# An encoder layer on one core: the experts' weights moved from the streamed to the split side of the matmuls

## The chip, the core and the metric

The kernel runs on one core of one Trainium2 chip. The metric is the device time of one execution in microseconds, the median of three runs. A core has five engines that work in parallel and meet at semaphores: TensorE (PE in the profile, with its weight loads as PEld), VectorE (DVE), ScalarE (ACT), GpSimd (POOL) and SyncE (SP), which here only issues transfers. In a matmul one operand is loaded into the array (stationary) and the other streams through it (moving). PSUM has eight banks of 128 x 512 float32.

## The reference, cut to what matters

One layer of an encoder for 1024 tokens of width 1024: RMSNorm, input projection, three token mixers, output projection, RMSNorm, then a mixture of 32 experts of which each token uses two, and a final RMSNorm. Only the experts are touched by the change:

```
def hierarchical_moe(h, rg_w, rg_b, re_w, re_b, e_gate, e_up, e_down):
    ...
    for e in range(N_EXPERTS):
        y = (jax.nn.silu(t @ e_gate[e]) * (t @ e_up[e])) @ e_down[e]
        out = out + combine[:, e:e + 1] * y
```

`t` is 1024 x 1024; `e_gate[e]` and `e_up[e]` are 1024 x 256, `e_down[e]` is 256 x 1024, all float32, 3 MB an expert.

## The kernel before, in words

Input projection, mixers and output projection come first. The output projection's rows are normalised (`normalise2`, L1223, one call for each of 8 tiles of 128 tokens), stored to HBM as `h2_rows`, transposed and multiplied with the router's weights `rw`. VectorE makes from the router's result two lists, `tok` and `dest`, with 80 slots (`CAP`) for each expert; unused slots point out of bounds and move nothing, so an expert has 64 rows on average (2 x 1024 / 32). An overflow path for experts with more than 80 rows follows the loop and is skipped when there are none.

Then the experts. The first four are written out, the other 28 run in loops of four (`Fori`) on every engine. For expert e:

- GpSimd copies a column of `tok` into `tokc` (L1584) and gathers up to 80 rows into `xg` (L1586). A column of `dest` is copied (L1597) and `ysb` is scattered to `y_d` (L1599) three experts behind.
- SyncE fetches the weights into a ring of four places: `wg`, `wu` when `gate_up` of the expert four before is done, `wd` when its `down` is done. Each 1 MB is one transfer. In `wg` and `wu` partition p holds rows p, 128+p, ...: eight pieces of 1 KB in HBM. In `wd` a piece is 4 KB.
- TensorE transposes the rows (`ex_transposes`, L759, 8 instructions), runs `down_split` of expert e-2 and then `gate_up` of e (L768). `gate_up` is in plain float32: the weights are stationary, 32 blocks of 128 x 128, and the 96 columns of `xT` move; each such product is two matmul instructions in the profile (64 for an expert). `down_split` works with split operands: float32 w is taken as w_hi + w_lo, both of type float32r, and hi x hi, hi x lo and lo x hi are summed. That is 12 instructions with an 80-column stationary `hThi_e` or `hTlo_e` and 512 moving columns of `wdhi` or `wdlo` (L787, L788, L792).
- ScalarE copies `xT` (L1016), half of the result rows (L1047), casts `wd` to `wdhi` (L1036, 2048 elements a partition) and does the Silu (L1020). VectorE copies the other half (L1380), makes `wdlo` = `wd` - `wdhi` (L1388), the gated product (L1372) and its two parts (L1394, L1396).

After the last scatter SyncE loads all rows of `y_d` back, VectorE adds them (L1421), and the final norm and the stores end the program.

## Time and profile before

| what | us |
|---|---|
| median of three runs (894.12 to 897.29) | 895.49 |
| the profiled execution: its own time | 892.98 |
| the profiled execution: span from first to last instruction | 891.0 |
| first row transposes of the experts to the last result in PSUM (L759 at 498.4, L792 ends at 841.8) | 343.4 |

The span starts at the first instruction and leaves out some 2 us around it. The profile's page gives busy time by engine, the granted TensorE clock in tenths of full speed, and the chain that ended last; the trace gives single instructions by start and length, what an engine waited for before them, and bandwidth by stretch. Matmuls are pipelined: the length of one (393 ns for L788) overlaps the next, and the distance of their starts is what one costs.

### The profile page before, as it was taken

The numbers are of one execution on the slowest core, as the hardware profiler recorded it, in microseconds if no ns is written. First come the engines' busy times: TensorE is split into PE (matmuls) and PEld (weight loads), VectorE is DVE, ScalarE is ACT, GpSimd is POOL, SyncE is SP. The second block draws the span as 40 slices with busy tenths as digits, with TensorE's granted clock in tenths as the row PEclk, the third lists the DMA queues.
The fourth block names the chain that finished last, engine by engine and source line by source line (L and its number), as shares of the span: only waits on it lengthen the run. The fifth ranks groups of instructions, "written<-read, shape, count | busy, mean of one in ns | idle before, by whom it ended". The sixth has DMA issues, their size and how long they took to land.

```text
span 891.0 us, 13079 instructions
## 1 busy us (share of the span) xinstructions
PE 771.9 (87%) x5022; PEld 641.3 (72%) x5022; DVE 373.1 (42%) x767; ACT 302.0 (34%) x539; POOL 329.7 (37%) x313
## 2 busy tenths in 40 slices
PE   3999999999977888999973599999999999999700
PEld 2788888866654554787873599999998899999600
DVE  5540000046768885412238233343333333333266
ACT  6211112145558887202220233333333333333222
POOL 2432256435556771501110123443433333442134
PEclk9999999979999999999995699999999999999955
DMA  8451112000010002426358189999999999996194
GB/s 273 108 151 48 47 48 71 1 0 1 2 48 0 1 1 76 137 69 219 113 172 300 38 258 335 351 349 351 348 349 350 347 342 347 350 352 231 40 370 195
DMA packets 111238, 160.21 MB, mean 180 GB/s; under 512 B 8304, under 2 KB 88656, under 8 KB 111072
## 3 DMA queue, kind: packets, MB, share of 16 engines
q1 hardware_dynamic: 104800, 142.78, 47.9%
q0 software_dynamic: 6400, 16.92, 5.9%
q8 instruction: 25, 0.41, 0.2%
q14 instruction: 13, 0.11, 0.0%
HBM read 144.99 MB, written 18.87 MB: 184 GB/s over the span
## 4 chain that ended last, share of the span: by engine, by line
PE 75%; DVE 9%; ACT 6%; DMA 4%; issue 3%; POOL 1%; SPq 1%; POOLq 0%; ACTq 0%; DVEq 0%
PE ps L768 26%; PE ps L583 6%; PE ps L585 6%; PE ps L584 6%; PE ps L788 3%; PE ps L787 3%; PE ps L792 3%; PE ps L623 3%; PE ps L759 2%; PE ps L648 2%; PE ps L707 2%; PE ps L709 2%; PE ps L708 2%; PE ps L664 2%; PE ps L670 2%
## 5 line engine op out<-in xcount | busy, mean ns | idle before, releaser
L768 PEld LDWEIGHTS ps<-xT,wg 128*128 128x128 f32 x1024 | 121.6, 195 | 5.9 <-ACT xT L1016 2.3
L768 PE MATMUL ps<-xT,wg 128*128 128x96 f32 x1024 | 121.4, 278 | 1.8 <-ACT xT L1016 1.8
L768 PE MATMUL ps<-xT,wu 128*128 128x96 f32 x1024 | 119.6, 275 | 0.0
L768 PEld LDWEIGHTS ps<-xT,wu 128*128 128x128 f32 x1024 | 116.9, 192 | 0.0
L1388 DVE TENSOR_TENSOR wdlo<-wd,wdhi 128x2048 fp32r<-128x2048 f32 x32 | 73.4, 2292 | 63.0 <-ACT wdhi L1036 63.0
L583 PE MATMUL ps<-hThi,whi 128*128 128x512 f32 x224 | 88.3, 394 | 4.2 <-DVE hTlo L1086 4.2
L585 PE MATMUL ps<-hThi,wlo 128*128 128x512 f32 x224 | 87.7, 392 | 0.0
L584 PE MATMUL ps<-hTlo,whi 128*128 128x512 f32 x224 | 87.7, 391 | 0.0
L1584 POOL COPY tokc<-tok 80x1 int32 (+1 forms) x32 | 54.1, 1689 | 42.7 <-DVE tok L1369 30.7
L1597 POOL COPY destc<-dest 80x1 int32 (+1 forms) x32 | 5.7, 178 | 166.7 <-DVE ysb L1380 166.7
L1536 POOL TENSOR_SCALAR pswa<-pswa,esum 128x384 f32<-128x384 f32 (+1 forms) x48 | 55.5, 1165 | 31.8 <-DVE esum L1173 31.4
L1020 ACT ACTIVATE sg<-ps 128x192 f32<-128x192 f32 x32 | 10.6, 330 | 154.2 <-PE ps L768 154.2
L1036 ACT CAST wdhi<-wd 128x2048 fp32r<-128x2048 f32 x32 | 60.7, 1897 | 0.0
L707 PE MATMUL ps<-wohi,oThi 128*128 128x512 f32 x128 | 50.9, 397 | 4.0 <-DVE oTlo L1205 3.6
L583 PEld LDWEIGHTS ps<-hThi,whi 128*128 128x128 f32 x224 | 42.4, 189 | 13.3 <-issue 4.7
L787 PE MATMUL ps<-wdhi,hThi_e 128*80 128x512 f32 x128 | 52.0, 406 | 0.0
L788 PE MATMUL ps<-wdlo,hThi_e 128*80 128x512 f32 x128 | 50.3, 393 | 0.0
L1372 DVE TENSOR_TENSOR hT<-sg,ps 128x192 f32<-128x192 f32 x32 | 11.4, 356 | 92.7 <-ACT sg L1020 92.7
L1153 DVE CUSTOM_DVE_ANT_0 pna<-ps,te 128x512 f32<-128x512 f32 x16 | 10.9, 688 | 93.6 <-PE ps L623 93.4
L709 PE MATMUL ps<-wohi,oTlo 128*128 128x512 f32 x128 | 49.9, 390 | 0.0
L708 PE MATMUL ps<-wolo,oThi 128*128 128x512 f32 x128 | 49.9, 390 | 0.0
L1380 DVE COPY ysb<-ps 80x512 f32<-80x512 f32 x32 | 22.0, 686 | 66.4 <-PE ps L792 66.4
(194 smaller groups left out, 1415.4 us busy)
## 6 DMA issues: line engine op xcount, KB each, us to landing
wg<-in_expert_w_gate SPq DMA_DIRECT2D x32, 1024.0 KB, 8.9
wu<-in_expert_w_up SPq DMA_DIRECT2D x32, 1024.0 KB, 12.7
wd<-in_expert_w_down SPq DMA_DIRECT2D x32, 1024.0 KB, 6.0
y<-expert_rows SPq DMA_DIRECT2D x16, 512.0 KB, 9.5
wraw<-in_w_in SPq DMA_DIRECT2D x14, 512.0 KB, 3.9
xin<-in_x SPq DMA_DIRECT2D x8, 512.0 KB, 5.6
xres<-in_x SPq DMA_DIRECT2D x16, 256.0 KB, 3.0
h_rows<-h SPq DMA_DIRECT2D x8, 512.0 KB, 2.7
```

What stands on the lines that cost most here:

```text
L583: nc.tensor.matmul(bank, whi[i % 2][:, k, :], hThi[:, k, cols], start=(k == 0), stop=False)
L584: nc.tensor.matmul(bank, whi[i % 2][:, k, :], hTlo[:, k, cols], start=False, stop=False)
L585: mm = nc.tensor.matmul(bank, wlo[i % 2][:, k, :], hThi[:, k, cols], start=False, stop=(k == KT - 1))
L707: nc.tensor.matmul(ps[:, g % 4, :], oThi[:, k, rows], wohi[n][:, k, :], start=(k == 0), stop=False)
L708: nc.tensor.matmul(ps[:, g % 4, :], oThi[:, k, rows], wolo[n][:, k, :], start=False, stop=False)
L709: mm = nc.tensor.matmul(ps[:, g % 4, :], oTlo[:, k, rows], wohi[n][:, k, :], start=False, stop=(k == KT - 1))
L768: mm = nc.tensor.matmul(ps[:, bank, f * COLS:(f + 1) * COLS], w[:, k, c0:c0 + P], xTu[:, k, :], start=(k == 0), stop=(k == KT - 1))
L787: nc.tensor.matmul(ps[0:CAP, b0 + n, :], hThi_e[par][:, j, :], wdhi[par][:, j, cols], start=(j == 0), stop=False)
L788: nc.tensor.matmul(ps[0:CAP, b0 + n, :], hThi_e[par][:, j, :], wdlo[slot][:, j, cols], start=False, stop=False)
L1036: nc.scalar.copy(wdhi[u % 2][:], wd[u][:]).then_inc(wdhi_done, 1)
L1388: nc.vector.tensor_tensor(wdlo[u][:], wd[u][:], wdhi[u % 2][:].bitcast(F32), ALU.subtract).then_inc(wdlo_done, 1)
L1536: gp.tensor_scalar(pbuf(u), pbuf(u), esum[:, u:u + 1], None, ALU.mult).then_inc(norm_p, 1)
```

## The change

The experts are written out, without loops, and all products are split:

- `gate_up`: the rows are stationary now, as `xThi` and `xTlo` (80 columns), and gate and up weights move together, 256 columns of each, into one bank. Three products for each of 8 chunks of k make 24 matmuls of 512 columns. The result has the tokens on partitions, so the gated product `hx` is transposed (`h_rows`, two instructions) ahead of `down`.
- The weights' high parts are cast by ScalarE into four units of 8 KB (`unit`): two for the halves of gate and up (`half_high`, chunks 0 to 3 and 4 to 7) and one for `wd` (`down_high`). `half_high(e, 0)` waits for `down` of e-3, `half_high(e, 1)` for the first half of `gate_up(e-1)`, `down_high(e)` for `gate_up(e)`. VectorE makes the low parts in the place of the raw weights (`half_low`, `down_low`).
- `down` runs one expert behind instead of two. ScalarE copies the whole result, 80 x 1024 (`rows_out`).
- d_model is laid out as 8p + k over partition p and chunk k: `e_gate` and `e_up` come in one piece of 8 KB for each partition, `rw` likewise, and `normalise2` writes its row permuted, reading with a step of 8 elements.
- GpSimd uses `tok` and `dest` directly as indices; no copies of columns.

The core of the diff:

```diff
-        wg = [at(f"wg{i}", [P, KT, DE], F32, eoff[i]) for i in range(RING)]
-        wu = [at(f"wu{i}", [P, KT, DE], F32, eoff[i] + 8 * KB) for i in range(RING)]
+        wgu = [at(f"wgu{i}", [P, 2, KT, DE], F32, eoff[i]) for i in range(RING)]
+        wgulo = [at(f"wgulo{i}", [P, 2, KT, DE], F32R, eoff[i]) for i in range(RING)]
         wd = [at(f"wd{i}", [P, 2, D], F32, eoff[i] + 16 * KB) for i in range(RING)]
+        wdlo = [at(f"wdlo{i}", [P, 2, D], F32R, eoff[i] + 16 * KB) for i in range(RING)]
+        unit = [at(f"unit{i}", [P, 2, 4 * DE], F32R, off) for i, off in enumerate((H + 56 * KB, W + 56 * KB, H + 24 * KB, V))]
...
+        xThi = [at(f"xThi{i}", [P, KT, CAP], F32R, TMP + 2560 * i) for i in range(2)]
+        xTlo = [at(f"xTlo{i}", [P, KT, CAP], F32R, (TMP + 5120, W + 53 * KB)[i]) for i in range(2)]
+        sg = at("sg", [CAP, DE], F32, TD + 32 * KB)
+        hx = at("hx", [COLS, DE], F32, TD + 33 * KB)
+        hThi_e = at("hThi_e", [P, 2, CAP], F32R, TD + 34 * KB)
+        hTlo_e = at("hTlo_e", [P, 2, CAP], F32R, TD + 34 * KB + 640)
...
+        def weight_unit(e, part):
+            return unit[(3 * e + (0, 1, 5)[part]) % 4]
+        def raw_half(w, e, a):
+            return w[e % RING][:, :, 4 * a:4 * a + 4, :].rearrange("p g k f -> p g (k f)")
...
-            sp.dma_start(rw[:, :, N_GROUPS:NR], re_w[0].rearrange("(k p) n -> p k n", p=P)).then_inc(const_in, 16)
+            sp.dma_start(rw[:, :, 0:N_GROUPS], rg_w[0].rearrange("(p k) n -> p k n", p=P)).then_inc(const_in, 16)
+            sp.dma_start(rw[:, :, N_GROUPS:NR], re_w[0].rearrange("(p k) n -> p k n", p=P)).then_inc(const_in, 16)
...
-                return (g_src.rearrange("(k p) f -> p k f", p=P), u_src.rearrange("(k p) f -> p k f", p=P),
+                return (g_src.rearrange("(p k) f -> p k f", p=P), u_src.rearrange("(p k) f -> p k f", p=P),
...
-            def fetch_expert(e, u, dynamic=False):
-                a, b, c = load_expert(e, u, dynamic)
-                if dynamic:
-                    sp.wait_ge(gu_done, e - (RING - 1))
-                sp.dma_start(wg[u][:], a).then_inc(wgu_in[u], 16)
-                sp.dma_start(wu[u][:], b).then_inc(wgu_in[u], 16)
-                if dynamic:
-                    sp.wait_ge(down_done, e - (RING - 1))
+            def fetch_expert(e):
+                u = e % RING
+                a, b, c = load_expert(e, u, False)
+                if e >= RING:
+                    sp.wait_ge(half_done, 2 * (e - RING) + 2)
+                sp.dma_start(wgu[u][:, 0], a).then_inc(wgu_in[u], 16)
+                sp.dma_start(wgu[u][:, 1], b).then_inc(wgu_in[u], 16)
+                if e >= RING:
+                    sp.wait_ge(down_done, e - RING + 1)
                 sp.dma_start(wd[u][:], c).then_inc(wd_in[u], 16)
...
+            def x_rows(e):
+                pe.wait_ge(xg_in[e % 2], 16 * (e // 2 + 1))
+                if e >= 1:
+                    pe.wait_ge(xThi_done, e)
+                    pe.wait_ge(xTlo_done, e)
+                rows_transposed(xg[e % 2]).then_inc(etr_done, 1)
...
+            def gate_up(e):
+                bank = ps[0:CAP, 2 + e % 2, :].rearrange("q (g f) -> q g f", g=2)
+                pe.wait_ge(xThi_done, e + 1)
+                if e >= 2:
+                    pe.wait_ge(hThi_done, e - 1)
+                    pe.wait_ge(hTlo_done, e - 1)
+                for a in range(2):
+                    hi, lo = weight_unit(e, a), raw_half(wgulo, e, a)
+                    pe.wait_ge(ahi_done, 2 * e + a + 1)
+                    for k in range(4):
+                        nc.tensor.matmul(bank, xThi[e % 2][:, 4 * a + k, :], hi[:, :, k * DE:(k + 1) * DE],
+                                         start=(a == 0 and k == 0), stop=False)
+                    if a == 0:
+                        pe.wait_ge(xTlo_done, e + 1)
+                    for k in range(4):
+                        nc.tensor.matmul(bank, xTlo[e % 2][:, 4 * a + k, :], hi[:, :, k * DE:(k + 1) * DE], start=False, stop=False)
+                    pe.wait_ge(alo_done, 2 * e + a + 1)
+                    for k in range(4):
+                        mm = nc.tensor.matmul(bank, xThi[e % 2][:, 4 * a + k, :], lo[:, :, k * DE:(k + 1) * DE],
+                                              start=False, stop=(a == 1 and k == 3))
+                    mm.then_inc(half_done, 1)
...
+            def h_rows(e):
+                pe.wait_ge(h_made, e + 1)
+                for j in range(2):
+                    mm = nc.tensor.transpose(ps[:, 2 + e % 2, j * COLS:(j + 1) * COLS], hx[:, j * P:(j + 1) * P], ident[0:COLS, 0:COLS])
+                mm.then_inc(htr_done, 1)
...
+            def down(e):
+                b0 = 4 + 2 * (e % 2)
+                hi = weight_unit(e, 2)[:].rearrange("p a f -> p (a f)").rearrange("p (j d) -> p j d", j=2)
+                pe.wait_ge(dhi_done, e + 1)
+                pe.wait_ge(hThi_done, e + 1)
+                if e >= 2:
+                    pe.wait_ge(y_out, e - 1)
...
+            x_rows(0)
+            for e in range(N_EXP):
+                if e >= 1:
+                    h_rows(e - 1)
+                if e + 1 < N_EXP:
+                    x_rows(e + 1)
+                gate_up(e)
+                if e >= 1:
+                    down(e - 1)
+            h_rows(N_EXP - 1)
+            down(N_EXP - 1)
...
+            def half_high(e, a):
+                u = 3 * e + a
+                if a == 0:
+                    act.wait_ge(wgu_in[e % RING], 32 * (e // RING + 1))
+                if a == 0 and e >= 3:
+                    act.wait_ge(down_done, e - 2)
+                if a == 1 and e >= 1:
+                    act.wait_ge(half_done, 2 * (e - 1) + 1)
+                nc.scalar.copy(weight_unit(e, a)[:], raw_half(wgu, e, a)).then_inc(ahi_done, 1)
+            def down_high(e):
+                act.wait_ge(wd_in[e % RING], 16 * (e // RING + 1))
+                act.wait_ge(half_done, 2 * e + 2)
+                nc.scalar.copy(weight_unit(e, 2)[:], wd[e % RING][:].rearrange("p j d -> p (j d)").rearrange("p (a f) -> p a f", a=2)
+                               ).then_inc(dhi_done, 1)
...
+            act.wait_ge(tok_done, 2)
+            half_high(0, 1)
+            x_high(0)
+            for e in range(N_EXP):
+                if e >= 1:
+                    h_high(e - 1)
+                if e + 1 < N_EXP:
+                    x_high(e + 1)
+                    half_high(e + 1, 0)
+                    half_high(e + 1, 1)
+                if e >= 2:
+                    rows_out(e - 2)
+                silu(e)
+                down_high(e)
+            h_high(N_EXP - 1)
+            rows_out(N_EXP - 2)
...
-                nc.vector.scalar_tensor_tensor(out=h2[t % 2][:], in0=x1[:, t, :], scalar=stat[:, 3, t:t + 1], in1=gbc[:],
+                nc.vector.scalar_tensor_tensor(out=h2[t % 2][:].rearrange("q (k p) -> q k p", k=KT),
+                                               in0=x1[:, t, :].rearrange("q (p k) -> q k p", k=KT), scalar=stat[:, 3, t:t + 1],
+                                               in1=gbc[:].rearrange("q (p k) -> q k p", k=KT),
...
+            def half_low(e, a):
+                dve.wait_ge(ahi_done, 2 * e + a + 1)
+                nc.vector.tensor_tensor(raw_half(wgulo, e, a), raw_half(wgu, e, a), weight_unit(e, a)[:].bitcast(F32),
+                                        ALU.subtract).then_inc(alo_done, 1)
...
+            half_low(0, 0)
+            half_low(0, 1)
+            x_low(0)
+            for e in range(N_EXP):
+                if e >= 1:
+                    h_low(e - 1)
+                if e + 1 < N_EXP:
+                    x_low(e + 1)
+                    half_low(e + 1, 0)
+                    half_low(e + 1, 1)
+                gated(e)
+                down_low(e)
+            h_low(N_EXP - 1)
...
+            def scatter(e):
+                pool.wait_ge(y_out, e + 1)
+                gp.indirect_dma_start(y_d, bass.IndirectOffsetOnAxis(ap=dest[:, e:e + 1].bitcast(U32), axis=0), ysb[e % 2][:], None,
+                                      bounds_check=bound(bound_y, 2 * S - 1), oob_is_err=False).then_inc(y_put[e % 2], 16)
+            gather(0)
+            gather(1)
+            for e in range(N_EXP):
+                if e + 2 < N_EXP:
+                    gather(e + 2)
+                if e >= 3:
+                    scatter(e - 3)
+            for e in range(N_EXP - 3, N_EXP):
+                scatter(e)
```

TensorE in the loop, one expert. Before, from `gate_up` of one expert over the transposes of the next to the middle of a `down_split`:

```order
L768 MATMUL ps<-xT_187,wg_148 128x96 x16
L768 MATMUL ps<-xT_187,wu_152 128x96 x16
L759 MATMUL ps<-ident,xg_184 128x96 x8
L787 MATMUL ps<-wdhi_160,hThi_e_178 80x512
L788 MATMUL ps<-wdlo_162,hThi_e_178 80x512
L787 MATMUL ps<-wdhi_160,hThi_e_178 80x512
L788 MATMUL ps<-wdlo_162,hThi_e_178 80x512
L792 MATMUL ps<-wdhi_160,hTlo_e_180 80x512 x2
L787 MATMUL ps<-wdhi_160,hThi_e_178 80x512
```

And now, from `h_rows(e-1)` over `x_rows(e+1)` and `gate_up(e)` into `down(e-1)`:

```order
L805 MATMUL ps<-ident,hx 128x96 x2
L768 MATMUL ps<-ident,xg_176 128x96 x8
L790 MATMUL ps<-unit_164,xThi_179 80x512 x4
L795 MATMUL ps<-unit_164,xTlo_181 80x512 x4
L798 MATMUL ps<-wgulo_154,xThi_179 80x512 x4
L790 MATMUL ps<-unit_165,xThi_179 80x512 x4
L795 MATMUL ps<-unit_165,xTlo_181 80x512 x4
L798 MATMUL ps<-wgulo_154,xThi_179 80x512 x4
L817 MATMUL ps<-unit_166,hThi_e 80x512 x2
L821 MATMUL ps<-unit_166,hTlo_e 80x512 x2
L825 MATMUL ps<-wdlo_161,hThi_e 80x512 x2
```

`x16` on L768 is two instructions each in the profile. The 32 products of plain float32 became 24 split ones, two transposes stand ahead, and `down` stands behind `gate_up` instead of ahead of it.

ScalarE in the loop, one expert, before (copy of `xT`, half of the rows, cast of `wd`, Silu):

```order
L1016 COPY xT_187<-ps 128x768 [waits gu_done,etr_done]
L1047 COPY ysb_183<-ps 80x512 [waits y_put1,down_done]
L1036 CAST wdhi_161<-wd_156 128x2048 [waits down_done,wd_in1]
L1020 ACTIVATE sg_175<-ps 128x192 [waits gu_done]
L1025 REGISTER_ALU
L1016 COPY xT_186<-ps 128x768 [waits gu_done,etr_done]
```

And now (high part of the hidden rows, of the next expert's rows, two half casts of the next expert, result rows, Silu, cast of `wd`):

```order
L1078 CAST hThi_e<-ps 128x160 [waits down_done,htr_done]
L1070 CAST xThi_178<-ps 128x640 [waits half_done,etr_done]
L1049 CAST unit_163<-wgu_147 128x2048 [waits down_done,wgu_in0]
L1049 CAST unit_164<-wgu_147 128x2048 [waits half_done]
L1093 COPY ysb_175<-ps 80x1024 [waits y_put1,down_done]
L1085 ACTIVATE sg<-ps 80x256 [waits h_made,half_done]
L1055 CAST unit_165<-wd_158 128x2048 [waits half_done,wd_in3]
```

One cast of 2048 elements became three, and the Silu stands behind two of them.

VectorE in the loop, from one result copy or hidden-row step to the next, before:

```order
L1380 COPY ysb_183<-ps 80x512 [waits y_put1,down_done]
L1387 REGISTER_ALU
L1388 TENSOR_TENSOR wdlo_163<-wd_156,wdhi_161 128x2048 [waits wdhi_done]
L1372 TENSOR_TENSOR hT_177<-sg_175,ps 128x192 [waits down_done,silu_done]
L1394 CAST hThi_e_179<-hT_177 128x160 [waits h_made]
L1396 TENSOR_TENSOR hTlo_e_181<-hT_177,hThi_e_179 128x160 [waits hT_done]
```

And now:

```order
L1454 TENSOR_TENSOR hTlo_e<-ps,hThi_e 128x160 [waits hThi_done]
L1446 TENSOR_TENSOR xTlo_181<-ps,xThi_179 128x640 [waits xThi_done]
L1433 TENSOR_TENSOR wgulo_152<-wgu_148,unit_166 128x2x1024 [waits ahi_done]
L1433 TENSOR_TENSOR wgulo_152<-wgu_148,unit_163 128x2x1024 [waits ahi_done]
L1462 TENSOR_TENSOR hx<-sg,ps 80x256 [waits htr_done,silu_done]
L1439 TENSOR_TENSOR wdlo_159<-wd_155,unit_164 128x2048 [waits dhi_done]
```

One subtraction of 2048 elements became three; the gated product stands behind those of the next expert.

## Rows read from the trace of the kernel before

**Rows 1.** The page: busy us by engine, share of the span, instructions.

```profile
PE 771.9 (87%) x5022; PEld 641.3 (72%) x5022; DVE 373.1 (42%) x767; ACT 302.0 (34%) x539; POOL 329.7 (37%) x313
```

**Rows 2.** Chain of waits, one expert of the loop: start us, length us, what.

```profile
646.33 0.66 PE ps L759 x8
...
649.77 7.12 PE ps L768 x64
656.89 0.66 PE ps L759 x8
```

**Rows 3.** The same chain in the input projection.

```profile
60.35 0.23 PE ps L583
...
61.03 0.23 PE ps L583
```

**Rows 4.** Timeline beside that expert: start us, length, what [idle before].

```profile
650.71 0.18 POOL L1597 COPY destc<-dest 80x1 int32 x1 [4.95 <-DVE ysb L1380]
650.90 1.37 SPq L503 DMA_DIRECT2D wu<-in_expert_w_up  x1
651.69 0.94 POOL L1599 DMA_INDIRECT expert_rows<-ysb,destc  x1 [0.81 <-POOL destc L1597]
652.22 2.29 DVE L1388 TENSOR_TENSOR wdlo<-wd,wdhi 128x2048 fp32r<-128x2048 f32 x1 [1.73 <-ACT wdhi L1036]
652.63 1.92 POOL L1584 COPY tokc<-tok 80x1 int32 x1
```

**Rows 5.** Groups by line and shape, 500 to 891 us: busy, mean ns of one.

```profile
L1388 DVE TENSOR_TENSOR wdlo<-wd,wdhi 128x2048 fp32r<-128x2048 f32 x32 | 73.4, 2292 | 63.0 <-ACT wdhi L1036 63.0
L1036 ACT CAST wdhi<-wd 128x2048 fp32r<-128x2048 f32 x32 | 60.7, 1897 | 0.0
...
L1016 ACT COPY xT<-ps 128x768 f32<-128x768 f32 x32 | 25.6, 801 | 42.5 <-PE ps L759 42.5
...
L1380 DVE COPY ysb<-ps 80x512 f32<-80x512 f32 x32 | 22.0, 686 | 66.4 <-PE ps L792 66.4
...
L1047 ACT COPY ysb<-ps 80x512 f32<-80x512 f32 x32 | 18.6, 581 | 63.7 <-PE ps L792 63.7
L1372 DVE TENSOR_TENSOR hT<-sg,ps 128x192 f32<-128x192 f32 x32 | 11.4, 356 | 92.7 <-ACT sg L1020 92.7
```

**Rows 6.** Stretches: us, busy of PE, PEld, DVE, ACT, POOL, clock, DMA share, GB/s.

```profile
462.00:482.00 20.00, 3.80 (x20) 3.19 (x19) 15.41 (x67) 0.44 (x2) 0.63 (x1) 0.58 1.07 365
466.00:470.00 4.00, 0.00 (x0) 0.00 (x0) 3.52 (x15) 0.21 (x1) 0.00 (x0) 0.50 1.05 386
540.00:640.00 100.00, 100.00 (x793) 90.46 (x792) 36.76 (x49) 33.47 (x40) 36.22 (x37) 1.00 1.03 348
...
850.00:870.00 20.00, 0.00 (x0) 0.00 (x0) 16.46 (x14) 4.62 (x9) 8.96 (x8) 0.50 1.02 405
```

**Rows 7.** The page's DMA issues: KB each, median us from issue to landing.

```profile
wu<-in_expert_w_up SPq DMA_DIRECT2D x32, 1024.0 KB, 12.7
```

**Rows 8.** Chain of waits where the experts begin.

```profile
498.43 1.55 PE ps L759 x8
...
500.86 9.94 PE ps L768 x64
...
522.71 0.46 PE ps L792 x2
```

**Rows 9.** Chain of waits where they end.

```profile
841.78 0.70 DVE ysb L1380
...
842.61 0.19 POOL destc L1597
```

**Rows 10.** Timeline of the last normalised tile and one router step.

```profile
456.16 1.28 DVE L1223 SCALAR_TENSOR_TENSOR h<-x,stat,gbc 128x1024 f32<-128x1024 f32 x1 [2.36 <-POOL stat L1467]
...
458.89 1.07 PE L719 MATMUL ps<-ident,h 128*128 128x128 f32 x8
...
465.53 0.60 DVE L1284 TENSOR_REDUCE rs<-rt 128x64 f32<-128x256 f32 x1
```

More of the change, by code:

```diff
@@ new lines, in down @@
+                    if n == 0:
+                        pe.wait_ge(dlo_done, e + 1)
+                    for j in range(2):
+                        mm = nc.tensor.matmul(ps[0:CAP, b0 + n, :], hThi_e[:, j, :], wdlo[e % RING][:, j, n * 512:(n + 1) * 512],
+                                              start=False, stop=(j == 1))
+                mm.then_inc(down_done, 1)
+            pe.wait_ge(hx_zero, 1)
+            x_rows(0)
[7 more added lines that the diff above has]
+                    down(e - 1)
```

288 lines of the change are left out of this document (100 added, 188 removed).

## The prediction

> **What bounds the kernel now.** First the page: TensorE is busy 87% of the span and nothing else over 42%, so the question is whether it ever waits in the experts [rows 1]. The chain of waits answers: through the loop it is TensorE alone. One expert is 0.66 us of row transposes, 2.78 us of `down_split` and 7.12 us of `gate_up`, and the next starts 10.56 us after the one before, which is the sum, with no gap [rows 2]. So in the loop only TensorE's own work counts, until something else becomes longer than it. Two candidates: the transfers, which move 348 GB/s there at a share of 1.03 [rows 6], and ScalarE and VectorE, which each get two more passes over 2048 elements.
>
> **TensorE's sum.** The 12 matmuls of `down_split` take 2.78 us, 0.231 each [rows 2]. The new `gate_up` has the same form (80 stationary columns, 512 moving ones, split parts): 24 x 0.231 = 5.54 us for 7.12. What differs is that the 512 columns are two runs of 256, which no row shows; I take it as free, since the 128-column form of the projection costs 0.227 (0.68 for three) [rows 3], which is also the lower bound. The two new transposes cost 2 x 0.66 / 8 = 0.17. An expert becomes 0.17 + 0.66 + 5.54 + 2.77 = 9.14 us: 1.42 less than 10.56. At 0.227 for all 36 it would be 9.00.
>
> **ScalarE and VectorE.** From the groups [rows 5], ScalarE's copy costs 0.14 us + 0.86 ns an element (512 take 581 ns, 768 take 801), VectorE's 0.16 us + 1.03 ns (512 and 192 from PSUM take 686 and 356). ScalarE: three casts at 1.90, `x_high` (640) 0.69, `rows_out` (1024) 1.02, `h_high` (160) 0.28, Silu (256) 0.36, together 8.05. VectorE: three subtractions at 2.29, `x_low` 0.82, `gated` 0.42, `h_low` 0.32, together 8.43. Both are under 9.14, but order counts, so I lay one expert out from the start of `h_rows(e-1)` at 0. TensorE: row transposes end at 0.83, first half of `gate_up(e)` at 3.60, all of it at 6.37, `down(e-1)` at 9.14. ScalarE: `h_high` and `x_high` to 1.6, first cast for e+1 to 3.5, the second needs the first half (3.60) and ends at 5.5, `rows_out` to 6.6, Silu 6.6 to 7.0, `down_high` to 8.9. VectorE: low parts of e+1 from 3.5 to 5.8 and on to 8.1, `gated` to 8.5, `down_low` from 8.9 to 2.1 of the next turn, where `h_low` and `x_low` follow to 3.3. `gated` is needed at 9.14: 0.6 us of room. So the added casts, subtractions and waits cost nothing as long as these lengths hold; if `gated` ends more than 0.6 us later, `h_rows` waits on it with everything behind it on TensorE.
>
> **The transfers.** An expert moves 348 GB/s x 10.56 us = 3.67 MB (3.15 of weights, the rest rows). At 9.14 us that is 402 GB/s. Rows for what the transfers can do: 365 over 20 us and 386 over 4 us while the first experts' weights come in, in pieces of 1 and 4 KB and paced by no engine; 405 when the rows come back at the end, all 4 KB [rows 6]. After the change the weights are pieces of 4 and 8 KB, so it is nearest to the last. It need not be met in full: weights for e+1 are asked for when `down(e-4)` ends, at the start of turn e-2, and cast from 1.6 us into turn e, 19.9 us later. Now `wu` lands 12.7 us after issue [rows 7] and is issued 1.1 after the `down` that both `wd` and it come behind (650.90 against 649.77) [rows 2, 4]: 13.8, so 6.1 us may be lost over 28 experts, 0.22 each. A transfer period up to 9.36 us (392 GB/s) costs nothing; 386 GB/s (9.51) costs 28 x 0.15 = 4, 365 (10.05) costs 19. I take nothing, nearer to 405, and keep the others for the range.
>
> The Trainium skill (DMA: Bandwidth & Descriptors, "Where 436 GB/s comes from") says that HBM gives a core about 358 GB/s and that this binds for HBM to SBUF. By that an expert would take 10.25 us and the change would win 25 us less. The 386 and 405 of this trace are above it [rows 6], so I give it a small chance only.
>
> **The other edits.** GpSimd loses two copies of a column for each expert and keeps a gather (wanted two turns later) and a scatter; nobody waits for them in the loop. `normalise2` reads with a step of 8 elements. The nearest row is a reduction that reads 256 elements with that step in 0.60 us [rows 10]: four times that, 2.4 us, bounds the 1.28 of now, so up to 1.1 more, eight times. For seven tiles TensorE is in the output projection; for the last, 456.16 + 2.4 = 458.6, and its transposes start at 458.89 anyway. Cost 0, bound 1. The gather's wait behind `half_low` is below.
>
> **Start.** Before, the first row transposes end at 499.98 and the first `down` at 523.17 [rows 8]; the first `gate_up` took 9.94 for 7.12 us, 2.8 lost at half clock. Now `x_high` and `x_low` come one after the other (501.5), the transposes for expert 1 at half clock (1.55) stand ahead of `gate_up(0)`: 503.1. With the same 2.8 lost it ends at 511.4. The casts for expert 1 wait for its first half (508.2), so the last subtraction ends at 512.4 and `gated` at 512.8; transposes to 513.7, `gate_up(1)` to 519.2, `down(0)` to 522.0. That is 1.2 earlier.
>
> One thing comes ahead of all that. GpSimd's copy of a column takes 0.18 us alone and 1.92 when it starts under VectorE's `wdlo`; it ends when that ends (654.5) [rows 4]. The new first gather is issued just when `half_low(0, 0)` starts. Either it runs through, as the scatter of these rows did when `wdlo` started under it (up to 0.2 us gained, the copy), or it waits for one subtraction (1.4 later) or for two (3.7). The copy is the nearest row, as it starts under VectorE too: +1.4. The Trainium skill (SBUF — State Buffer, "SBUF: two separate sides") has a lock there: VectorE with two SBUF inputs and a GpSimd instruction that reads SBUF exclude each other for the whole of the one that came first. The copy's 1.92 us agrees, `wdlo` beside the running scatter does not; by the rule the +1.4 or the 3.7 holds and rival 2 could come true.
>
> **End.** Thirty turns of 9.14, the last without row transposes, bring `down(30)` to 522.0 + 274.2 - 0.7 = 795.5. The last `down` waits: `gate_up(31)` ends at 792.8, Silu 793.2, `down_high` 795.1, `down_low` 797.4, `h_low` 797.8, and ten matmuls are left: 800.1, where it was 841.78 [rows 9]. ScalarE alone copies the result: 1.02 for 0.70, and the 0.19 of the column's copy goes [rows 9]: +0.1.
>
> **Sum.** 800.1 - 841.8 + 0.1 + 1.4 = -40.2 us. The span goes from 891.0 to about 851, the profiled execution's own time from 892.98 to 853. That execution was 2.5 us below the median of the three; taken off the median it gives 895.49 - 40 = 855.5.
>
> **The rivals.** (1) *The transfers become the bound.* For: share 1.03 at 348 GB/s already, rows are gathered and scattered in between, and 402 is at the highest rate seen. Against: the pieces are larger, and `wu` lands well ahead of its use. Price 4 to 19 us beyond the room: 859 to 875. By the page's 358 it is 880. (2) *Slower than before: VectorE is held up by GpSimd.* The lock seen in the copy would work the other way round: two indirect transfers of 0.94 us for an expert, each with VectorE shut out. VectorE would need 8.43 + 0.3 of handovers + 1.9 = 10.65 us, and as it now feeds every `gate_up`, the period would be that: 30 x 1.51 = 45 on top, 901. It decides from about 0.4 us of hold-up an expert, and the time is above the old one from 1.7. Against: `wdlo` started 0.5 us into the scatter's 0.94 and took its 2.29 all the same [rows 4], and its mean over 32 is 2292 ns [rows 5]. (3) *Faster still:* 0.227 a matmul and no hold-up of the first gather: 30 x 0.14 + 1.6 = 6 less, 850. That the change doesn't do what it says is no rival: the order shows the 24 products.
>
> **Chances.** TensorE bound as summed, 852 to 859: 0.60. Transfers bound, 859 to 877: 0.19; at 358 GB/s, about 880: 0.05. VectorE or ScalarE late: 0.09, half of it below 880 and half about or above the old time. Below 852: 0.07. The range is 849 to 877. A measurement here can tell some 0.3% from no change, 2.7 us: faster 0.93, same 0.02, slower 0.05.
>
> **What will show it.** Right: starts of the row transposes 9.1 to 9.2 us apart through the loop, 0.23 us between `gate_up`'s matmuls, TensorE's waits under 0.2 us an expert, 395 to 405 GB/s. Wrong in the matmuls: over 0.24 us apart. Wrong in the transfers: ScalarE's first cast waiting on `wgu`, more from expert to expert, at a rate below 392 GB/s. Wrong in the engines: `h_rows` waiting on `gated`, or subtractions longer than 2.29 us. Wrong at the start: the first gather's landing far from 499.8.

## The result, and the profile after

The changed kernel takes 871.3 us (median of 4 runs, 868.6 to 874.3) where the kernel before takes 895.0 on the same chip: ratio 0.973, 95% interval 0.970 to 0.977. That is 23.7 us less. The forecast was 855.5, 40 less; the time is inside the range of 849 to 877, but in the part that belonged to rival 1, which had a chance of 0.19; the sum itself missed by 16 us. A second measurement of the same kernel on another chip gave 869.8, ratio 0.972 (0.969 to 0.975).

The page of the profiled execution (its own time 868.6, span 866.7). First the busy line, which answers [rows 1]:

```profile
PE 729.9 (84%) x3806; PEld 528.7 (61%) x3806; DVE 514.3 (59%) x800; ACT 436.4 (50%) x635; POOL 299.2 (35%) x249
...
PE 56%; DMA 17%; DVE 13%; ACT 8%; issue 3%; SPq 1%; POOL 1%; POOLq 0%; DVEq 0%; ACTq 0%
DMA wgu<-in_expert_w_up 13%; PE ps L592 6%; PE ps L594 6%; PE ps L593 6%; PE ps L790 4%; PE ps L795 4%; PE ps L798 4%; PE ps L632 3%; DVE wgulo L1433 3%; PE ps L657 2%; PE ps L716 2%; PE ps L718 2%; PE ps L717 2%; PE ps L673 2%; PE ps L821 2%
```

The last two lines are the page's chain, by engine and by line. 13% of the span is one kind of transfer, the weights of `gate_up`. Where in the loop it comes in is told by the chain in order of time (start us, length us, what). It answers [rows 2, 8, 9]; lines 790, 795 and 798 are the three products of `gate_up`, 817 to 825 those of `down`, 768 the row transposes:

```profile
499.54 1.53 PE ps L768 x8
...
514.21 1.71 PE ps L790 x4
...
523.66 0.66 PE ps L768 x8
524.33 0.92 PE ps L790 x4
525.25 0.92 PE ps L795 x4
526.16 0.92 PE ps L798 x4
...
532.75 0.66 PE ps L768 x8
...
596.36 0.66 PE ps L768 x8
...
605.73 0.47 SPq L514
606.24 21.75 DMA wgu<-in_expert_w_up
628.01 1.92 ACT unit L1049
629.95 1.84 DVE wgulo L1433
632.16 2.28 DVE wgulo L1433
635.21 0.66 PE ps L768 x8
...
645.09 22.75 DMA wgu<-in_expert_w_up
...
675.06 0.66 PE ps L768 x8
...
714.79 0.66 PE ps L768 x8
...
755.43 0.66 PE ps L768 x8
...
795.17 0.66 PE ps L768 x8
...
817.14 1.02 ACT ysb L1093
```

Read it in three pieces. From 523.66 to 596.36 the chain is TensorE alone and an expert takes 72.70 / 8 = 9.09 us, with 0.92 us for four matmuls (0.23 each): the forecast's mechanism at the forecast's size. At 604 us it turns into a cycle with a transfer in it: `fetch_expert` issues the weights (L514), they land 22 to 24 us later, ScalarE casts, VectorE subtracts, TensorE multiplies, and the end of `down` (L825) lets SyncE, which waits for it, go on to the next fetch. From 635.21 to 755.43 there are three such rounds of four experts, 120.22 / 12 = 10.02 us an expert. ScalarE copies the last result out at 817.14, where it was 841.78 [rows 9].

The stretches (length, busy us of PE, PEld, DVE, ACT and POOL with counts, granted clock, transfer share, GB/s), to be held beside [rows 6]:

```profile
462.00:482.00 20.00, 3.55 (x17) 2.94 (x16) 15.65 (x68) 0.62 (x3) 0.91 (x2) 0.58 1.01 416
520.00:540.00 20.00, 20.00 (x102) 13.46 (x101) 17.96 (x13) 16.50 (x16) 3.64 (x4) 1.00 0.77 281
540.00:600.00 60.00, 60.00 (x308) 40.64 (x307) 52.52 (x41) 50.30 (x46) 17.10 (x14) 1.00 1.02 373
640.00:740.00 100.00, 93.03 (x462) 60.56 (x460) 80.29 (x60) 76.59 (x71) 30.17 (x20) 1.00 1.01 371
```

The share is 1.01 and more in three of the four: the transfer engines always have a packet on the way (the times of the packets are summed, so the share can pass 1). That alone doesn't say that they can't move more; the waits below do. With only weights on the way the rate is 416 GB/s (462 to 482; it was 365 before; the other runs with this layout have 399 to 416 there). In the loop, where gathered and scattered rows run beside them, it is 371 to 373, although TensorE would need 402. From 540 to 600 TensorE is busy all the time because it lives on the lead; by 604 that is used up.

Who waits, from 530 to 800 (engine and line, for whom, us in total, times, longest):

```profile
DVE wgulo L1433 <- ACT unit L1049: 43.4, 28, 2.6
...
ACT unit L1049 <- DMA wgu<-in_expert_w_up: 27.1, 21, 2.1
PEld ps L805 <- DVE hx L1462: 22.0, 20, 1.8
PE ps L805 <- DVE hx L1462: 13.0, 19, 1.4
```

It is the sign that the prediction named for a miss in the transfers: ScalarE's first cast waits for `wgu`, 1.3 us each time, and the wait is handed down to VectorE and at last to TensorE at the transposes of `hx` (L805).

### The profile page after: what moved, and what is told of

The parts are those of the page before. It is cut to its first block, busy times and chain, and to the rows that moved or that the text cites. A ratio compares the mean times of both kernels' runs of the same rounds, so it can differ in the third digit from the quotient of the medians.

```text
span 866.7 us, 10276 instructions
## 1 busy us (share of the span) xinstructions
PE 729.9 (84%) x3806; PEld 528.7 (61%) x3806; DVE 514.3 (59%) x800; ACT 436.4 (50%) x635; POOL 299.2 (35%) x249
## 4 chain that ended last, share of the span: by engine, by line
PE 56%; DMA 17%; DVE 13%; ACT 8%; issue 3%; SPq 1%; POOL 1%; POOLq 0%; DVEq 0%; ACTq 0%
DMA wgu<-in_expert_w_up 13%; PE ps L592 6%; PE ps L594 6%; PE ps L593 6%; PE ps L790 4%; PE ps L795 4%; PE ps L798 4%; PE ps L632 3%; DVE wgulo L1433 3%; PE ps L657 2%; PE ps L716 2%; PE ps L718 2%; PE ps L717 2%; PE ps L673 2%; PE ps L821 2%
## 5 line engine op out<-in xcount | busy, mean ns | idle before, releaser
L1433 DVE TENSOR_TENSOR wgulo<-wgu,unit 128x2048 fp32r<-128x2048 f32 x64 | 144.0, 2288 | 46.8 <-ACT unit L1049 46.7
L1049 ACT CAST unit<-wgu 128x2048 fp32r<-128x2048 f32 x64 | 120.2, 1910 | 56.4 <-DMA wgu<-in_expert_w_up 27.1
L1659 POOL DMA_INDIRECT expert_rows<-ysb,dest x32 | 52.0, 1624 | 170.6 <-ACT ysb L1093 162.1
L1439 DVE TENSOR_TENSOR wdlo<-wd,unit 128x2048 fp32r<-128x2048 f32 x32 | 73.4, 2292 | 5.6 <-ACT unit L1055 5.2
L790 PE MATMUL ps<-unit,xThi 128*80 128x512 f32 x256 | 72.8, 406 | 0.0
L1654 POOL DMA_INDIRECT xg<-h_rows,tok x32 | 38.6, 1205 | 95.8 <-PE ps L768 64.6
L795 PE MATMUL ps<-unit,xTlo 128*80 128x512 f32 x256 | 69.5, 393 | 0.0
L798 PE MATMUL ps<-wgulo,xThi 128*80 128x512 f32 x256 | 69.1, 391 | 0.0
L1055 ACT CAST unit<-wd 128x2048 fp32r<-128x2048 f32 x32 | 60.8, 1901 | 0.0
L795 PEld LDWEIGHTS ps<-unit,xTlo 128*80 128x80 f32 x256 | 38.3, 150 | 21.7 <-issue 0.9
```

The lines of the kernel that those rows point to most:

```text
L790: nc.tensor.matmul(bank, xThi[e % 2][:, 4 * a + k, :], hi[:, :, k * DE:(k + 1) * DE], start=(a == 0 and k == 0), stop=False)
L795: nc.tensor.matmul(bank, xTlo[e % 2][:, 4 * a + k, :], hi[:, :, k * DE:(k + 1) * DE], start=False, stop=False)
L798: mm = nc.tensor.matmul(bank, xThi[e % 2][:, 4 * a + k, :], lo[:, :, k * DE:(k + 1) * DE], start=False, stop=(a == 1 and k == 3))
L1049: nc.scalar.copy(weight_unit(e, a)[:], raw_half(wgu, e, a)).then_inc(ahi_done, 1)
L1433: nc.vector.tensor_tensor(raw_half(wgulo, e, a), raw_half(wgu, e, a), weight_unit(e, a)[:].bitcast(F32), ALU.subtract).then_inc(alo_done, 1)
L1439: nc.vector.tensor_tensor(wdlo[e % RING][:].rearrange("p j d -> p (j d)").rearrange("p (a f) -> p a f", a=2), wd[e % RING][:].rearrange("p ...
```

## Experiments

Each run is told against the kernel before on the same chip (894.2 to 894.3 us there); intervals are 95%.

### Are the rows the reason? Scatters, gathers, both left out

First the scatter's writes alone. A bound of 0 makes the transfer drop nearly every row; its instruction stays. The end reads other rows of the same size, since these were not written.

```diff
 def scatter(e):
-                          bounds_check=bound(bound_y, 2 * S - 1), oob_is_err=False).then_inc(y_put[e % 2], 16)
+                          bounds_check=bound(bound_y, 0), oob_is_err=False).then_inc(y_put[e % 2], 16)
```

> The changed kernel with every scatter issued as before but its bound set to 0, so that only a row with index 0 is written, and the last phase reads the normalised rows in place of the experts' rows (same sizes); its output leaves the experts' results out. 3.41 instead of 3.67 MB an expert. Theory A (the transfers bind from about 604 us on, and writing rows slows the weights' packets more than its bytes do): starts of the row transposes 9.09 us apart to the end, about 857 us, and a DMA share clearly under 1, near 0.92 at 375 GB/s. Theory B (bytes alone, the rate stays at 371 GB/s at share 1.01): 9.19 us apart, about 857 too, but with a share of 1.02. Theory C (not the transfers but ScalarE and VectorE's order sets 9.9 us): stays at 871.

Measured 851.5 us (851.0 to 854.1), ratio 0.953 (0.950 to 0.955).

Then the gather's reads alone, by the same bound; the experts work on rows that are left over from before.

```diff
 def gather(e):
-                          bounds_check=bound(bound_x, S - 1), oob_is_err=False).then_inc(xg_in[e % 2], 16)
+                          bounds_check=bound(bound_x, 0), oob_is_err=False).then_inc(xg_in[e % 2], 16)
```

> The changed kernel with every gather issued but its bound set to 0, so that only row 0 of the normalised rows is ever fetched and the experts work on stale rows; its output is not the reference's. 3.41 MB an expert. Theory A with the gather as the part that slows the weights' packets: 9.09 us apart to the end, about 857 us, DMA share near 0.92. If the scatter is that part, the share here stays near 1.0 at 375 GB/s. Theory B: 9.19 us apart, share 1.02. Theory C: 871.

Measured 852.0 us (851.4 to 853.4), ratio 0.953 (0.951 to 0.955).

And both edits at once.

> Both of the last two together: gathers and scatters issued, but no rows moved; its output leaves the experts out. 3.15 MB of weights an expert are left. Theory A and B: TensorE bound throughout, 9.09 us apart, first result to last as summed in the prediction, 855 to 857 us; DMA share 0.84 at 346 GB/s if the weights go as fast as at 462 to 482 us of the changed kernel (416 GB/s at share 1.01), 0.94 if they keep the loop's rate. Theory C: 871.

Measured 851.0 us (850.1 to 851.8), ratio 0.951 (0.949 to 0.953). The stretch from 640 to 740 us of the three, in that order, with the same columns:

```profile
640.00:740.00 100.00, 100.00 (x508) 67.55 (x507) 88.91 (x67) 85.11 (x78) 27.15 (x22) 1.00 1.02 374
```

```profile
640.00:740.00 100.00, 100.00 (x508) 67.54 (x507) 88.89 (x67) 85.13 (x78) 27.18 (x22) 1.00 0.98 373
```

```profile
640.00:740.00 100.00, 100.00 (x508) 67.54 (x507) 88.90 (x67) 85.11 (x78) 27.14 (x22) 1.00 0.90 347
```

In all three TensorE is busy for the whole 100 us and the kernel comes to the TensorE bound at 851 to 852. The casts, the subtractions and the instructions on GpSimd are all still there, so the time between 851 and 871 hangs on the rows that are moved, and not on the order of the engines' work. The times don't tell the gather from the scatter: either one gone is enough, and once TensorE is the bound, the GB/s column shows only what is asked for (374 and 373 with one kind of rows, 347 with none), not what the transfers could do. The traces' records of single packets tell more. From 640 to 740 us a weight packet of 8 KB takes 351 ns in the mean in the changed kernel, 335 with the gather alone beside it (e1), 323 with the scatter alone (e2) and 311 with neither (e3). The gather stretches them more than the scatter, which fits the shares, 1.02 for e1 and 0.98 for e2.

### The weights' layout

The gate and up weights go back to 1 KB pieces, `normalise2` and the router's weights to their old order with them; the split halves and the products stay.

```diff
-    return (g_src.rearrange("(p k) f -> p k f", p=P), u_src.rearrange("(p k) f -> p k f", p=P),
+    return (g_src.rearrange("(k p) f -> p k f", p=P), u_src.rearrange("(k p) f -> p k f", p=P),
...
-    nc.vector.scalar_tensor_tensor(out=h2[t % 2][:].rearrange("q (k p) -> q k p", k=KT),
+    nc.vector.scalar_tensor_tensor(out=h2[t % 2][:],
```

> The changed kernel with the old layout of d_model: gate and up weights in pieces of 1 KB, router weights and normalised rows as before, no reads with a step. Everything else as changed. If the size of the pieces sets the rate: the loop runs at 350 to 360 GB/s, 10.2 to 10.5 us an expert instead of 9.9, binds earlier, and the kernel takes 880 to 890 us, so that most of the gain is gone. If the pieces do not matter beside the rows: 371 GB/s and 871 us.

Measured 889.8 us (887.2 to 893.8), ratio 0.996 (0.994 to 0.998).

Then the other half alone: the kernel before with the new layout and its own products.

> The kernel before with the new layout of d_model alone: gate and up weights in pieces of 8 KB, router weights likewise, normalised rows written permuted with reads at a step of 8; products, casts and loops as before. If TensorE bounds that loop, as summed in the prediction, it stays at 10.56 us an expert and the kernel within 0.3% of before (893 to 896), with the DMA share falling from 1.03 to about 0.97. If the loop before was at the edge of the transfers after all, it gets faster by some us.

Measured 894.8 us (894.1 to 898.5), ratio 1.001 (0.999 to 1.002). Stretches of e4 (first line) and e8:

```profile
640.00:740.00 100.00, 87.94 (x433) 57.48 (x434) 75.39 (x58) 70.17 (x66) 28.70 (x20) 0.98 1.06 344
```

```profile
640.00:740.00 100.00, 100.00 (x803) 91.41 (x803) 37.68 (x47) 33.55 (x38) 39.04 (x39) 1.00 0.94 345
```

With 1 KB pieces the transfers reach their end at 344 GB/s (share 1.06), the rate of the kernel before (348 at 1.03) [rows 6]. Eight packets of 1 KB take 8 x 54 = 430 ns there, where one of 8 KB takes 351. The jam reaches SyncE as well. Its issues in e4 (start, length):

```profile
650.14 5.81 SPq L515 DMA_DIRECT2D wgu<-in_expert_w_up  x1
656.00 4.37 SPq L518 DMA_DIRECT2D wd<-in_expert_w_down  x1
```

In the changed kernel either takes 0.4 us; in e4 it is 2.6 to 7.2 from 563 to 714 us, and the chain runs through them all that time. It isn't the price of issuing 1 KB pieces as such: the kernel before has them too, and `wu` is issued in 0.5 to 3.2 us there (1.37 in [rows 4]). The shorter products alone bring 0.4%; the layout alone brings nothing and only lowers the share, 1.03 to 0.94; together they bring 2.7%. The kernel before stood within some 1% of a second bound while TensorE was its first, and neither half of this change pays without the other. e4 also says what the forecast's reading of [rows 6] was missing: in the loop the old layout gave 344, and it gave 365 where only weights came in. The new one gives 371 and 416. The gap between the two stretches is there in both layouts.

### The order of the fetches

SP waits for `down` before it fetches `wd`, and the next expert's `wgu` stands behind that wait. Here `wd` is issued one expert later, after the next `wgu`.

```diff
-    if e >= RING:
-        sp.wait_ge(down_done, e - RING + 1)
-    sp.dma_start(wd[u][:], c).then_inc(wd_in[u], 16)
+    if e < RING:
+        sp.dma_start(wd[u][:], c).then_inc(wd_in[u], 16)
...
 for e in range(1, N_EXP):
     fetch_expert(e)
+    if e - 1 >= RING:
+        fetch_down(e - 1)
+fetch_down(N_EXP - 1)
```

> The changed kernel with SyncE's list of transfers reordered: the gate and up weights of expert e+1 are asked for as soon as gate_up of e-3 is done, ahead of the down weights of e, which wait for down of e-4, 2.8 us later in each turn. Nothing else changes. If the loop is bound by the transfers' rate once their lead is used up, 9.9 us an expert stays as it is in the late loop, and the only gain is that the saturated stretch begins up to 2.8 us earlier: 868 to 870 us. If it were bound by latency (a request that comes too late each turn), each turn would gain: 9.09 us throughout and 851 us.

Measured 864.1 us (861.8 to 864.6), ratio 0.964 (0.962 to 0.967): the fastest kernel here that computes the reference whole, and 0.9% below the changed kernel. Its stretches:

```profile
520.00:540.00 20.00, 20.00 (x101) 13.45 (x100) 18.33 (x14) 16.45 (x15) 3.49 (x3) 1.00 0.87 322
...
640.00:740.00 100.00, 95.25 (x473) 62.32 (x471) 81.72 (x61) 78.60 (x73) 29.85 (x21) 1.00 1.00 371
```

The rate in the loop is the same 371, so this is no cure, but the kernel starts with more lead: 322 GB/s instead of 281 in the first 20 us, where the share was only 0.77, and ScalarE waits for `wgu` 14 times (18.3 us) instead of 21 (27.1). The chain leaves TensorE at 640 us and not at 604. The changed kernel wasted transfer time at the start while SP stood at a wait.

### The gather's place in SBUF

If the rows and the weights' packets meet at some part of SBUF because the 80 rows lie on neighbouring partitions, placing them apart should help. e6 gathers 32 rows to partitions 0 to 31 and 48 rows to partitions 64 to 111; e7 is its control, in two transfers as well, but the second goes to partitions 32 to 79, where its rows were before (32 for 64 in the first added line).

```diff
 def gather(e):
-    gp.indirect_dma_start(xg[e % 2][0:CAP, :], None, h2_d, bass.IndirectOffsetOnAxis(ap=tok[:, e:e + 1].bitcast(U32), axis=0),
+    for r0, r1, d0 in ((0, 32, 0), (32, CAP, 64)):
+        gp.indirect_dma_start(xg[e % 2][d0:d0 + r1 - r0, :], None, h2_d,
+                              bass.IndirectOffsetOnAxis(ap=(tok2 if r0 else tok)[0:r1 - r0, e:e + 1].bitcast(U32), axis=0),
```

> As the control, but rows 32 to 79 go to partitions 64 to 111 and TensorE transposes 112 rows in place of 96; ScalarE and VectorE take the 80 used columns in two pieces. If the gather slows the weights because its 64 rows an expert all lie in partitions 0 to 63 (writes to few ports of SBUF), this spreads them over both halves: packets of the gather back near 160 ns, 390 GB/s or more possible, the loop bound by TensorE again at 9.2 us (0.11 more for the transposes), 853 to 858 us. If the gather's cost is its reads from HBM or its count of packets: 370 GB/s, 9.9 us late in the loop, 871 to 873.

Measured 883.9 us (882.0 to 887.1), ratio 0.988 (0.986 to 0.991).

> Control for the next one: each gather of 80 rows issued as two, rows 0 to 31 and 32 to 79, to the same partitions as before (the second with a list of its own that VectorE copies once). Same bytes, same places, one more transfer an expert. Expected by both theories: 871 us within 2, 370 GB/s in the loop, the gather's 4 KB packets 186 to 210 ns.

Measured 876.3 us (874.0 to 878.2), ratio 0.978 (0.975 to 0.981). From 640 to 740 us e6 has 362 GB/s, the control 367, the changed kernel 371. So this placing doesn't help; it costs 7.6 us beside its control. That sum includes two costs that aren't the transfers': `x_high` and `x_low` became two instructions each, and TensorE transposes 112 rows instead of 96. Splitting alone may cost some 5, though the intervals of e7 and the changed kernel touch. The idea fell in this form only: each of e6's two transfers is narrow, 32 and 48 partitions, and none reaches over all of SBUF.

### Is it that rows are gathered by indices?

A plain transfer of 64 neighbouring rows of `h_rows` takes the place of the gather. The experts then work on rows that aren't theirs, here and in the next run.

```diff
-    gp.indirect_dma_start(xg[e % 2][0:CAP, :], None, h2_d, bass.IndirectOffsetOnAxis(ap=tok[:, e:e + 1].bitcast(U32), axis=0),
-                          bounds_check=bound(bound_x, S - 1), oob_is_err=False).then_inc(xg_in[e % 2], 16)
+    r = 30 * e
+    pool.dma_start(xg[e % 2][0:64, :], h2_d[r:r + 64, :]).then_inc(xg_in[e % 2], 16)
```

> The changed kernel with each gather by indices replaced by a plain transfer of 64 consecutive rows of the normalised rows, issued by GpSimd to the same partitions; the experts work on the wrong rows. Same bytes within 2%, same queue. If it is the gather by indices (its scattered rows or its list) that stretches the weights' packets from 311 to 350 ns, they are back near 325 here, the loop reaches 385 GB/s or more, and the kernel takes 852 to 860 us. If any second stream of rows into SBUF does it, 868 to 874.

Measured 873.7 us (870.2 to 875.5), ratio 0.976 (0.973 to 0.980), 366 GB/s in the loop. So the indices, the scattered reads and GpSimd's list aren't the reason.

### The same rows over all partitions

The same plain transfer with the same bytes, but each row written as two halves on two partitions: 128 x 2 KB where e9 has 64 x 4 KB.

```diff
-    pool.dma_start(xg[e % 2][0:64, :], h2_d[r:r + 64, :])
+    pool.dma_start(xg[e % 2][:, 0:512], h2_d[r:r + 64, :].rearrange("r (b f) -> (r b) f", b=2))
```

> As e9_plain_gather, a plain transfer of 64 consecutive rows of h_rows by GpSimd in place of the gather by indices, but written as 128 partitions x 2 KB (each row in two halves) instead of 64 partitions x 4 KB; the bytes are the same 0.26 MB. The experts work on rows that aren't theirs, so the experts' numbers are not the reference's; the work and the scatters are the same. Theory A, it matters how many partitions the rows are spread over (a narrow stream sits on a part of what the weights' packets also need): the loop's rate goes from 366 in 640:740 to 385 GB/s or more, TensorE is busy for all 100 us there, 851 to 856 us. Theory B, any second stream of these bytes beside the weights does it, whatever its shape: 366 to 373 GB/s again, 868 to 875 us.

Measured 849.9 us (846.3 to 852.5), ratio 0.949 (0.945 to 0.952). e9 (first line) beside e12:

```profile
640.00:740.00 100.00, 91.06 (x453) 59.34 (x452) 79.20 (x58) 76.23 (x70) 23.66 (x20) 1.00 1.01 366
```

```profile
640.00:740.00 100.00, 100.00 (x508) 67.51 (x507) 88.89 (x67) 85.13 (x78) 22.44 (x22) 1.00 1.01 404
```

The loop moves 404 GB/s, what TensorE asks for (3.67 MB in 9.09 us), and the kernel is back at its TensorE bound, with all the bytes on the way; ScalarE doesn't wait for `wgu` once between 530 and 800 us. The share is 1.01 at 404 as it is at 366, so the share by itself doesn't tell a loop that is held up by its transfers from one that isn't. The transfers' view of the same 100 us shows how. Its rows are GB/s in 40 slices of 2.5 us, then the two queues: packets, MB, share of the transfer engines' time (q1 carries the weights, q0 the rows). First e9, then e12:

```profile
GB/s 410 265 362 413 416 272 379 408 410 316 346 410 413 323 303 393 421 336 331 385 411 379 300 369 419 397 292 401 405 359 275 393 421 346 302 393 411 375 257 406
...
q1 hardware_dynamic: 5563, 31.30, 85.4%
q0 software_dynamic: 1748, 5.19, 15.8%
```

```profile
GB/s 428 400 406 419 424 331 416 426 418 370 418 437 364 362 431 416 387 416 428 375 359 408 436 369 388 431 436 383 421 428 392 401 418 431 362 362 421 441 385 423
...
q1 hardware_dynamic: 6164, 34.59, 86.5%
q0 software_dynamic: 1944, 5.74, 14.6%
```

Once an expert, every 10 us, e9 has a hole of one or two slices, down to 257 to 340 GB/s, between slices at 410. In e12 the holes are mostly at 360 to 390. In the same engine time the weights of e12 move more, too: 34.59 / 86.5 = 0.400 MB for a percent of the share, against 0.367 in e9. The packets of the two traces say the same: a weight packet of 8 KB takes 354 ns in the mean in e9 and 313 in e12, which still scatters; without any rows, in e3, it was 311. A row packet goes from 196 to 163 ns. So what stretches the transfers, the weights' among them, is the narrow shape of the second stream. Theory A of the expectation holds. Nor is it that smaller packets make way more easily: the trace has every row packet at 4 KB in both runs (1266 and 1402 of them), although each row is now written as two pieces of 2 KB. What isn't separated is the number of partitions from that halving within a packet; and why 64 or 80 partitions are bad, no run here shows.

### The start: the first gather behind a subtraction

`half_low(0, 0)` is moved ahead, among the router's steps, so that the first gather doesn't start under it; the fetch order is that of e5.

```diff
 step(v.tensor_tensor(gates[:, 1, :], gates[:, 0, :], s8(9), ALU.mult))
+half_low(0, 0)
 dve.wait_ge(rank_mm, 1)
...
-half_low(0, 0)
 half_low(0, 1)
```

> The reordered fetches of e5_fetch_order, and VectorE's subtraction half_low(0, 0) moved ahead of its wait for the rank matmul, out of the way of the first gather. If the first gather is slow (2.62 us for 0.95) because it starts under that subtraction, it takes about 1 us here and its rows land 1 to 1.7 us earlier; the router's steps behind lose 0.7 us or less. 0.5 to 1 us better than e5_fetch_order: 861 to 864 us, and 5 to 8 us below the changed kernel. If the gather's length has another cause, it stays at 2.6 us and the time is that of e5_fetch_order or 0.7 worse.

Measured 865.6 us (862.8 to 867.9), ratio 0.967 (0.964 to 0.970), no better than e5's 0.964.

e11 is the changed kernel unaltered, on the same chip.

> The changed kernel itself once more, beside the next two on one chip: 868 to 874 us, bound by TensorE at 9.09 us an expert until about 604 us and then by the transfers at 9.9.

Measured 869.8 us (866.9 to 871.5), ratio 0.972 (0.969 to 0.975). GpSimd's timeline at the first gathers (start, length, line, what, idle before), e11 first, then e10:

```profile
495.31 2.62 POOL L1654 DMA_INDIRECT xg<-h_rows,tok  x1 [31.20 <-DVE tok L1428]
498.24 1.71 POOL L1654 DMA_INDIRECT xg<-h_rows,tok  x1 [0.30 <-issue]
503.20 0.95 POOL L1654 DMA_INDIRECT xg<-h_rows,tok  x1 [3.25 <-PE ps L768]
```

```profile
497.78 1.14 POOL L1661 DMA_INDIRECT xg<-h_rows,tok  x1 [31.96 <-DVE tok L1442]
499.22 2.71 POOL L1661 DMA_INDIRECT xg<-h_rows,tok  x1 [0.30 <-issue]
```

The hold-up is real and can be moved: 2.62 us under the subtraction, 1.14 without it, and the rows land after 4.0 us instead of 5.5. But the subtraction's 2.3 us now stand before the router's lists, so the gather starts 2.5 us later and the first transposes are at 501.9 instead of 500.9. The wait was traded for the same work one step earlier, and the second gather (2.71) took it over.

## Why the prediction was right or wrong, point by point

**TensorE's turn: right.** 9.14 forecast, 9.09 measured. The matmuls whose 512 columns are two runs of 256 cost 0.23 each, as taken. Where the transfers don't bind (e1, e2, e3, e12), the kernel takes 849.9 to 852.0. The forecast, less the 0.05 us a turn for 30 turns, is 854.

**ScalarE and VectorE: right, as sizes and as an order.** The subtraction takes 2288 ns in the mean and the cast 1910. In the runs that TensorE bounds (e1, e2, e3, e12), TensorE is busy for 100.00 of 100 us, so `gated` is never late; the waits at `hx` above come after the cast's wait for `wgu`.

**The transfers: the step that failed.** The forecast's need was right (402 GB/s; e12 moves 404). The supply was not: the text took the changed weights as "nearest to the last" row, the 405 of the returning rows, and put the cost at nothing. That row, like the 365 and the 386, stands where one kind of transfer runs at a time, and the loop runs three. What speaks for the mix is the loop's own row, 348 at a share of 1.03, beside the 365 of the start: 17 GB/s less than weights alone with the same pieces, and e4 shows that 344 was indeed all it could do. The forecast noted the mix under rival 1 but gave it no price. Scaling by these two rows (348 / 365 of 405 is 386, at +4) would have halved the error in the rate, but given only 4 of the 16 us: with the new layout the gap is 45 GB/s, 416 alone and 371 in the loop, and no row of before showed that it would grow. What was wrong, then, was to let the middle of the sum stand on the upper end of 348 to 405 and give everything below 392 a chance of 0.19 and 0.05. The runs put 371 in its place, because the narrow stream of rows stretches the weights' packets (e9 against e12). The price list itself held: 365 GB/s was put at +19, and the loop at 371 gave +16.

The sum closes. The 20 turns from 596.36 to 795.17 take 9.94 us instead of 9.09, 17.0 more; the turn of 9.09 for 9.14 takes 1.5 back over 30: 15.5. The last result is copied at 817.14, where the forecast with its gather term had 801.5, 15.6 later; in e12 it is at 800.92.

The lead of 6.1 us was a right idea at about the right size: at 0.85 us lost a turn it should last 6.1 / 0.85 = 7 turns, and TensorE runs unhindered for nine from 523.66.

The rule that the prediction weighed, some 358 GB/s from HBM (the Trainium skill, DMA: Bandwidth & Descriptors, "Where 436 GB/s comes from"), isn't borne out as a bound on this core: weights alone came at 416, and of the 404 in e12 some 375 are reads from HBM (an estimate: 34.59 MB of weights and eleven times 0.26 MB of rows in 100 us). Its result of 880 was 9 us off, and for another cause.

**GpSimd and VectorE at the start: right in kind and nearly in size.** The first gather took 2.62 us on GpSimd (0.95 when free), and the first transposes start at 499.54 where they were at 498.43 [rows 8]: +1.1 for the +1.4 taken. The hold-up is that of one subtraction, the middle of the three cases.

**Rival 2, slower because VectorE is held: refuted.** The subtractions of the whole loop (line, times, shortest/median/longest ns) and the scatters that GpSimd issues:

```profile
L1433 DVE TENSOR_TENSOR wgulo<-wgu,unit x64: 2282/2291/2294, 493.2 to 800.9; 128x2048 fp32r<-128x2048 f32 x64
```

```profile
L1659 POOL DMA_INDIRECT expert_rows<-ysb,dest x32: 905/1808/1817, 530.8 to 818.9; - x32
```

In 64 subtractions the longest is 12 ns above the shortest, while the scatter's median doubles from its free 905 to 1808. One of them, at 643.36, starts under a subtraction that ends at about 644.3 and is done 0.9 us later; `wdlo`'s subtraction starts under it at 644.66 and takes its 2.29. The one who waits is GpSimd each time. The Trainium skill (SBUF — State Buffer, "SBUF: two separate sides") describes an exclusion that goes both ways, for the one that came first; only one direction of it is seen in these runs. GpSimd's waits cost nothing in the loop, since a gather is wanted two turns later.

**`normalise2`: cost nothing, as taken.** Its eight instructions (same columns), which took 1.28 us [rows 10], and who waited for them:

```profile
L1280 DVE SCALAR_TENSOR_TENSOR h<-x,stat,gbc x8: 2105/2206/2348, 410.0 to 455.9; 128x1024 f32<-128x1024 f32 x8
...
  PEld ps L728: 0.5, 1
```

The bound was 2.4 us, and 0.5 us of weight load in all is what it held up.

**The start and the clock: right in the sum, partly by luck.** `down(0)` ends at 523.5 (522.0 + 1.4 = 523.4 forecast). The steps between fit less well. The forecast had one stretch at half clock, with 2.8 us lost in `gate_up(0)`. There are two, each after TensorE had waited: granted clock 0.52 from 504.2 to 506.1 and 0.50 from 514.1 to 516.0, the lower level of 1.2 GHz, where four matmuls take 1.71 us for 0.92 at full clock. The first half of `gate_up(0)` ends at 507.96, 1.6 before its forecast (508.2 + 1.4), and the second stretch, which the forecast didn't have, takes that back.

**The end: right.** From the last copy to the end there is nothing that the forecast left out; the end is 15.6 us late because the loop is.

## What to carry to other kernels

When a change makes the bounding engine faster, look for the second bound at the rate of the same mix: a rate read where one kind of transfer runs alone is no supply for a loop in which three kinds run, and a share of 1.03 in the loop before is a reason to take its own rate as the upper end for these shapes until a run shows more. The share alone proves nothing (1.01 at 366 and at 404); a wait for the transfer does. A product that gets shorter and a layout that gets better may each be worth nothing alone (0.4% and 0.0% here) and 2.7% together; test both halves. If small row transfers run beside large weight loads, try their shape first: the same bytes over all 128 partitions instead of 64 were worth 24 us (e9 against e12, both on rows that aren't the experts'). For this kernel the next version would gather half rows over all partitions, with the order of e5; as 80 rows make 160 halves it needs two gathers and other transposes, and it wasn't tried.

## What the runs showed of the hardware that was not expected

- A stream of 0.26 MB an expert, beside 3.15 MB of weights and the scatters, lowers the whole rate from at least 404 to 366 GB/s when it is written 64 partitions x 4 KB, and not when it is written 128 x 2 KB; the weights' 8 KB packets take 354 and 313 ns. Moving 48 of 80 gathered rows to partitions 64 to 111 cost 8 us, copies and longer transposes included.
- Pieces of 8 KB instead of 1 KB raise the rate of weights alone from 365 to between 399 and 416 GB/s, and that of the mixed loop from 344 to 371.
- VectorE's subtraction with two SBUF inputs never waits for GpSimd's indirect transfers (2282 to 2294 ns, 64 times); they wait for it (0.95 to 2.62 us, 905 to 1808 ns).
- A VectorE instruction that reads two inputs of 1024 elements in steps of 32 bytes takes 2206 ns in the median where it took 1284.
- When the transfers jam, an issue of 1 MB holds SyncE for 3 to 7 us instead of 0.4 (e4).
